# Delta rule: the transposed T made by 32x32 block transposes on VectorE instead of by products on TensorE

## What is computed

```python
kb = kc * bc[..., None]
lower = jnp.where(strict, jnp.einsum('nbhid,nbhjd->nbhij', kb, kc) * decay, 0.0)
tmat = lax.linalg.triangular_solve(lower + eye, jnp.broadcast_to(eye, lower.shape),
                                   left_side=True, lower=True, unit_diagonal=True)
u = tmat @ (vc * bc[..., None])
w = tmat @ (kb * jnp.exp(gcum)[..., None])
```

## Time and profile before

| what | before |
|---|---|
| median of 3 runs | 1667.34 us (1666.53 to 1669.29) |
| the profiled execution's own time | 1668.22 us |
| its span, first to last instruction | 1666.4 us |
| TensorE busy | 1576.8 us, 95% of the span |
| VectorE busy | 784.0 us, 47% |
| ScalarE busy | 412.6 us, 25% |
| GpSimd busy | 228.4 us, 14% |
| mean granted TensorE clock | 0.962 |

### The profile page before, as it was taken

How to read it: one execution, slowest core, us unless ns; L and a number is a source line. 1 busy time by engine, 2 the same in 40 slices (tenths; PEclk the granted TensorE clock), 3 DMA queues, 4 the chain that set the end, 5 groups by cost and what they waited for, 6 DMA issues and landing times.

```text
span 1666.4 us, 32885 instructions
## 1 busy us (share of the span) xinstructions
PE 1576.8 (95%) x14052; PEld 1468.1 (88%) x14052; DVE 784.0 (47%) x1409; ACT 412.6 (25%) x710; POOL 228.4 (14%) x263
## 2 busy tenths in 40 slices
PE   7999999989998888898998999999999999999995
PEld 6899998989998646556878999999999999999995
DVE  6359787226665324555653334243342332423426
ACT  5312231222222114445553111111101111111112
POOL 4142000019773001110001000000000000000003
PEclk9999999999999568999998999999999999999998
DMA  6222111212221316025230111101111011011122
GB/s 203 69 42 54 39 40 39 63 52 79 80 82 39 98 19 190 2 77 170 84 102 28 62 39 51 64 26 51 39 52 64 28 49 57 33 64 39 39 102 103
DMA packets 114728, 108.76 MB, mean 65 GB/s; under 512 B 15292, under 2 KB 104839, under 8 KB 114568
## 3 DMA queue, kind: packets, MB, share of 16 engines
q1 hardware_dynamic: 87346, 93.37, 17.8%
q10 hardware_dynamic: 24006, 12.12, 2.7%
q0 software_dynamic: 3232, 1.17, 0.6%
HBM read 94.02 MB, written 12.93 MB: 64 GB/s over the span
## 4 chain that ended last, share of the span: by engine, by line
PE 48%; DVE 3%; ACT 2%; issue 1%; DVEq 0%
PE mf_ps L2604 29%; PE mf_ps L2611 15%; PE mf_ps L2564 3%; PE mf_ps L2592 1%; DVE h_lo L2430 1%; ACT h_hi L2327 1%; PE mf_ps L2632 0%; ACT mo_buf L214 0%; DVE mo_buf L2502 0%; DVE mo_x L2506 0%; ACT mo_buf L2384 0%; DVE ff_scaled L2474 0%; PE mf_ps L2574 0%; DVE ff_w_lo L2437 0%; DVEq L2239 0%
## 5 line engine op out<-in xcount | busy, mean ns | idle before, releaser
L2467 DVE TENSOR_TENSOR ff_acc<-ff_acc,mf_ps 128x344 f32<-128x344 f32 x264 | 135.4, 513 | 185.8 <-PE mf_ps L2611 185.6
L2604 PE MATMUL mf_ps<-h_lo,ff_w_hi 128*128 128x344 f32 x1008 | 213.8, 320 | 0.0
L2604 PE MATMUL mf_ps<-h_hi,ff_w_hi 128*128 128x344 f32 x1008 | 213.6, 320 | 0.0
L2604 PE MATMUL mf_ps<-h_hi,ff_w_lo 128*128 128x344 f32 x1008 | 212.7, 319 | 0.0
L2611 PE MATMUL mf_ps<-ff_h_hi,ff_d_hi 128*128 128x344 f32 x528 | 169.9, 322 | 2.0 <-issue 2.0
L2611 PE MATMUL mf_ps<-ff_h_hi,ff_d_lo 128*128 128x344 f32 x528 | 169.6, 321 | 0.0
L2604 PEld LDWEIGHTS mf_ps<-h_hi,ff_w_lo 128*128 128x128 f32 x1008 | 169.2, 188 | 0.0
L2604 PEld LDWEIGHTS mf_ps<-h_hi,ff_w_hi 128*128 128x128 f32 x1008 | 169.1, 188 | 0.0
L2611 PE MATMUL mf_ps<-ff_h_lo,ff_d_hi 128*128 128x344 f32 x528 | 168.9, 320 | 0.0
L2604 PEld LDWEIGHTS mf_ps<-h_lo,ff_w_hi 128*128 128x128 f32 x1008 | 168.8, 188 | 0.0
L2313 POOL TENSOR_TENSOR ff_x<-ff_x,ff_scaled 128x1024 f32<-128x1024 f32 x7 | 16.4, 2359 | 762.7 <-DVE ff_scaled L2474 762.7
(11 more groups left out here) (440 smaller groups left out, 2520.0 us busy)
## 6 DMA issues: line engine op xcount, KB each, us to landing
fs_keys<-in_cache_k_dram SPq DMA_DIRECT2D x64, 192.0 KB, 2.7
fs_values<-in_cache_v_dram SPq DMA_DIRECT2D x64, 192.0 KB, 2.6
ff_raw<-in_w_gate_dram SPq DMA_DIRECT2D x22, 512.0 KB, 3.9
ff_raw<-in_w_up_dram SPq DMA_DIRECT2D x22, 512.0 KB, 4.1
ff_d_raw<-in_w_down_dram SPq DMA_DIRECT2D x22, 512.0 KB, 5.6
in_raw<-in_w_in_dram ACTq DMA_DIRECT2D x20, 512.0 KB, 3.9
ld_x<-in_x_prompt_dram SPq DMA_DIRECT2D x8, 512.0 KB, 4.2
mo_o_raw<-in_w_out_dram SPq DMA_DIRECT2D x8, 512.0 KB, 5.1
```

Source lines behind the costliest of these rows:

```text
L2467: dve.tensor_tensor(part, part, ps[:, b, 0:TG], ALU.add).then_inc(down_added, 1)
L2604: last = pe.matmul(bank(t % 2 * 3 + g)[:, 0:TG], a[:, k], b[:, k, group(g)], start=(k == 0 and n == 0), stop=(k == KD - 1 and n == 2))
```

## The change

At levels 1 to 4 `next_t` no longer makes the update of the transpose. `add_level` adds the update of T alone (128x384), and a new step `turn_level` lets VectorE transpose the whole of `tt[s][:, 0]` into `tt[s][:, 1]` by blocks of 32x32. Up to the fifth level (lv = 4) T has nothing outside its diagonal blocks of 32, so this is its transpose. At level 5 the update of the transpose is still made by TensorE and added by VectorE, and that of T is still left out. The turns of both tiles are issued behind the adds of both. The first add that reads the GpSimd-made transpose no longer does so, though its wait stays. `next_t` waits for the turn of the level before (`t_turned`, one semaphore for each parity).

```diff
-                    if lv == 1:
-                        dve.wait_ge(t_added[s], of_level(c, 0))
-                        dve.wait_ge(tt_init[s], c // 2 + 1)
-                    else:
-                        dve.wait_ge(t_added[s], of_level(c, lv - 1))
-                    first = 0 if lv < LEVELS - 1 else 1
-                    mine = tt[s][:, first:2].rearrange("p k n t -> p k (n t)")
-                    dve.tensor_tensor(mine, mine, ps[:, 2 * s + first:2 * s + 2, 0:W], ALU.add).then_inc(t_added[s], 1)
+                    dve.wait_ge(t_added[s], of_level(c, lv - 1))
+                    if lv == 1:
+                        dve.wait_ge(tt_init[s], c // 2 + 1)
+                    if lv == LEVELS - 1:
+                        dve.wait_ge(t_turned[s], of_turn(c, lv - 1))
+                        dve.tensor_tensor(tt[s][:, 1], tt[s][:, 1], heads(2 * s + 1), ALU.add).then_inc(t_added[s], 1)
+                        return
+                    dve.tensor_tensor(tt[s][:, 0], tt[s][:, 0], heads(2 * s), ALU.add).then_inc(t_added[s], 1)
+
+                def turn_level(c, lv):
+                    s = c % 2
+                    dve.wait_ge(t_added[s], of_level(c, lv))
+                    flat = lambda k: tt[s][:, k].rearrange("p n t -> p (n t)")
+                    dve.transpose(flat(1), flat(0)).then_inc(t_turned[s], 1)
...
+                    if lo is not None and r > 0:
+                        turn_level(lo, r)
+                    if hi is not None and r + 3 < LEVELS - 1:
+                        turn_level(hi, r + 3)
                     if r > 0 and done is not None:
                         new_state(done, r - 1)
...
                     if lv == 1:
                         pe.wait_ge(tt_init[s], c // 2 + 1)
                         pe.wait_ge(q_copied, c + 1)
-                    if lv < LEVELS - 1:
-                        for n, e in pair_up:
-                            pe.matmul(heads(2 * s)[half(e), n], tt[s][half(e), 1, n], x[s][half(e), n], start=True,
-                                      stop=True)
+                    else:
+                        pe.wait_ge(t_turned[s], of_turn(c, lv - 1))
                     for n, e in pair_up:
-                        last = pe.matmul(heads(2 * s + 1)[half(e), n], x[s][half(e), n], tt[s][half(e), 1, n],
-                                         start=True, stop=True)
+                        if lv < LEVELS - 1:
+                            last = pe.matmul(heads(2 * s)[half(e), n], tt[s][half(e), 1, n], x[s][half(e), n], start=True,
+                                             stop=True)
+                        else:
+                            last = pe.matmul(heads(2 * s + 1)[half(e), n], x[s][half(e), n], tt[s][half(e), 1, n],
+                                             start=True, stop=True)
                     last.then_inc(tt_done[s], 1)
```

More of the change, by code:

```diff
@@ L1178, in delta_rule @@
              nc, ctx, *["dl_" + n for n in names])
-        slot_names = ("level_ready", "tt_init", "x_done", "tt_done", "x_copied", "t_added")
-        level_ready, tt_init, x_done, tt_done, x_copied, t_added = [
+        slot_names = ("level_ready", "tt_init", "x_done", "tt_done", "x_copied", "t_added", "t_turned")
+        level_ready, tt_init, x_done, tt_done, x_copied, t_added, t_turned = [
             semaphores(nc, ctx, *[f"dl_{n}{s}" for s in range(2)]) for n in slot_names]
@@ L1187, in delta_rule @@
         of_copy = lambda c, lv: c // 2 * (LEVELS - 1) + lv
+        of_turn = lambda c, lv: c // 2 * (LEVELS - 2) + lv
         def steps():
```

## The result

The changed kernel takes 1655.43 us (median of 4 runs, 1654.46 to 1659.2) against 1668.32 (4 runs); the ratio is 0.9933, with a 95% interval of 0.9909 to 0.9957. So it is 7 to 15 us faster, where 1646.8 was predicted and 1643 to 1655 given as the range. Two later measurements of the same kernel gave 1652.62 us, ratio 0.9905 [0.9876, 0.9933], and 1654.41 us, 0.9909 [0.9884, 0.9934]. The profiled execution took 1654.8 us, its span is 1653.0, 13.4 us under that of before.

The account below looks back on a forecast made before the run. TensorE's issue of small products was taken to bound the stage's middle. Fill 1.9, five periods 14.0, seventh 2.4 and eighth 2.2 gave 20.5 us off the 1667.34 median: 1646.8 us, range 1643 to 1655.

Parts of the forecast that it names:

- The walk through a period: Delta-rule stage: one period timed step by step without the four groups; TensorE sets 17.0 us, VectorE close behind, slack 0.1.
- Rival B: Turns on VectorE held up by GpSimd's instruction in flight; periods of 21.2 us, kernel slower at 1672.7 us; chance 0.05.
- Fill: Start of the stage: TensorE could be about 4.6 us earlier, but GpSimd's masks allow only 1.9 us gain.
- Third tile's period: First of five full periods from 401.14 us: four TensorE groups of 0.70 us go, 2.8 us gain.
- Four more full periods: The rest of the five full periods in the middle of the stage, each to gain 2.8 us.
- The seventh period and the drain: End of the stage: 2.4 us gain in the seventh period, 2.2 in the eighth from the last tile's levels 3 and 4.
- The turn at 0.55: VectorE's 128x384 transpose from SBUF to SBUF: taken at 0.55 us, with a start-to-start pitch of 0.47.
- rival A: Slow turns or VectorE's order make VectorE the bound, loop 14.0 + 4T plus about 0.6 of waits; 1651 to 1660 us; chance 0.18.
- rival D: VectorE's turns stretch GpSimd's 15.7 us to over 17; periods 17.5, 3 us less gain, 1650 us; inside the forecast's 0.68.
- a sign of being right: In the delta-rule stage, GpSimd's wait for L1522 (values and keys) was to be at 1 us or less.

Follow-up runs that it names:

- the wait for kept: Changed kernel with one more wait: at r = 1 GpSimd waits for the step's first kept before it masks; 1646.39 us, ratio 0.9882.
- few keys in one piece: Changed kernel with one of GpSimd's 24 key multiplications, the one running when the long kept arrives, cut to 8 of 384 columns; 1650.07 us.
- few keys: Changed kernel with GpSimd multiplying only 8 of the 384 columns of each page of keys, sample scores left wrong; 1646.23 us.
- the kernel before without kept: Kernel before the change, with kept and its add replaced by three fused state updates; 1668.8 us against 1668.93, ratio 1.0002.

## Why the prediction was wrong

**The main size missed, and its step.** The median of 1655.43 us lies 0.4 us above the range, and those of the two later measurements (1652.62, 1654.41) inside it, so on which side the number fell was luck; the mechanism had an error either way. The walk through a period had "v_new at 7.85, kept to 9.06": it gave kept the 0.94 us that it had in the middle of the trace before:

```profile
450.40 0.94 DVE L1375 TENSOR_TENSOR dl_kept<-state,dl_exps 128x192 f32<-128x192 f32 x1
```

That is the step that failed. In the third tile's period kept took 6.04 to 6.07 us in all three profiles of the changed kernel, and there the period was 21.3 to 23.4 us, not 17.0. The second kept of a period, 0.35 us in the loop of the prediction, took 1.2 in the middle ones. The prediction had a maximum of 1027 ns in 16 and no term for more. That was only the wait that the old order of the two queues happened to produce. Rival B had the right mechanism, a VectorE operation held by GpSimd's instructions in flight, but placed it on the new instruction and not on the one that the trace already showed to suffer from it. Of the Trainium skill's page named in the prediction (SBUF — State Buffer, section "SBUF: two separate sides") both halves fit what ran: the operation with two SBUF inputs is held, the turn and the reductions with one are not (528 to 579 ns, and 1336). But the Trainium skill's page speaks of the length of an instruction. Here the hold lasted over the rest of one and four more, until GpSimd's queue had a gap, and the measurement decides.

**Why only there.** In the fill GpSimd works without a pause and lies behind TensorE. In the third tile's period the changed order brings kept to it during a multiplication, 0.4 us before its end, with four more instructions ready behind. In later periods kept comes in the first mask and is let in after 0.6 us. Shown are the effect of a gap at this place (the wait for kept: 6.0 to 0.63 us), that of another moment of arrival (few keys in one piece: 1.10 us) and that the turns are not the cause (6.05 us without them). What decides whether kept gets in between two of GpSimd's instructions is not settled: it did so in the middle periods, and not at the four boundaries between 410.6 and 413.5. Neither the kind of instruction nor the moment of arrival decides it alone. In the last tile's period kept arrived 1.97 us into a multiplication of the same size, with the masks right behind it, and went in:

```profile
500.55 2.63 POOL L1288 TENSOR_TENSOR fs_keys<-fs_keys,dl_q_rows 128x1152 f32<-128x1152 f32 x1
...
502.52 0.87 DVE L1382 TENSOR_TENSOR dl_kept<-state,dl_exps 128x192 f32<-128x192 f32 x1
...
503.14 2.08 POOL L1280 TENSOR_TENSOR dl_level<-dl_lt,levels 128x384 f32<-128x384 f32 x2
```

In the second and third profiles it did so from 2.15 and 2.40 us into the multiplication there, where 2.25 us brought the long hold in the third tile's period.

**The sum by its terms**, against the second profile of the changed kernel. Fill: -1.9 forecast, -2.3 measured, and its reason is borne out (few keys: -4.4). Third tile's period: -2.8 forecast, +1.25 measured. Four more full periods: -11.2 forecast, -10.6 measured; they were 80.31 us, longer than the 19.8 each of the walk, and are now 17.4 each. The seventh period and the drain: -4.6 forecast, -5.1 measured. The opening: +1.5, with the first products at half clock, which was not in the sum. Together that is -15.2 against -20.5. The opening's part is no effect of the change, since the kernel before without kept has it too and one of the changed kernel's profiles has not. The first group of gram products in the result's profile, at half clock, and in one of kept on ScalarE, at full clock (it takes 2.82 us in the second profile of the changed kernel too, and 1.53 in the third):

```profile
369.97 2.82 PE L1511 MATMUL dl_ps<-proj 64*64 64x128 f32 x24 [1.16 <-DVE dl_beta_decay L1429]
```

```profile
369.27 1.53 PE L1518 MATMUL dl_ps<-proj 64*64 64x128 f32 x24 [1.16 <-DVE dl_beta_decay L1436]
```

**VectorE.** The turn at 0.55 (565 ns measured) and its single SBUF input were right, and so was rival A's loop, 14.0 + 4T and 0.6 of waits, once kept has its real times. With every turn twice T is 0.94 and kept takes 0.35 and 0.56 us instead of 0.94 and 0.35. That gives 13.6 + 3.8 + 0.6 = 18.0, and 17.94 was measured. In the changed kernel the loop holds kept at 0.60 and 1.19 us, and its period is 17.5 where TensorE alone needs 17.1. So VectorE sets the middle periods, by 0.4 us, and TensorE's waits for kd (2.3 us from 402 to 522) are the sign of it: rival A in a small form, by kept's second hold and not by a slow turn. Without the turns, and with kept on ScalarE, the period in the middle is 17.09.

**GpSimd, the transfers, the rest.** GpSimd is busy 15.71 us of a middle period, as before (15.70), so rival D did not come. (Its sum has a slip: four turns of 0.33 us on 15.7 make 17.0, not 17.5.) GpSimd's waits for the values fell only from 16.9 to 12.0 us, five waits of 2.4 each, where 1 us or less had been named as a sign of being right; it bound nothing in the middle all the same. The keys' pieces were never waited for. The forecast of 1646.8 is what the kernel takes once the hold is out of it: 1646.39, 1646.33 and 1646.19 us. That is no merit of the number. It fits with the other terms being of about the right size, as the sum by its terms shows more directly.

## What to carry to other kernels

An operation whose duration varies in the trace with the same shape (355 ns in the median, 1027 at most) may be waiting inside its busy time. When a change moves it against the other engine's queue, the longest duration seen so far is no bound; here it waited until that queue ran dry. In this kernel two remedies worked: the operation on ScalarE, or a wait on GpSimd that leaves a gap. At the critical place the wait cost GpSimd 0.3 us, and the hold had cost the period 4 to 6; elsewhere GpSimd had the slack for it.

## What the runs showed of the hardware

A 128x192 VectorE operation with both inputs in SBUF, 0.35 us at its shortest, took 6.04, 6.06 and 6.07 us in three profiles, over the end of one GpSimd instruction and four more, and ended 0.2 us after the last. At other places of the same kernel it went in between two GpSimd instructions (0.6 to 1.2 us). A block transpose of 128x384 float32 takes 528 to 579 ns, like an add of that size (552), and was not held by GpSimd at any of 32 places. The granted clock is not a property of the program: the stretch from 370 to 380 us ran at 0.50, 0.69 and 0.83 in three profiles of the changed kernel, and at 1.00 and 0.71 in two with kept on ScalarE. The opening was 1.3 to 1.7 us longer in those that had the first products at half clock, and a fall before the end of the drain cost another 2.5 us.
